# One transformer block with 32 experts on one core: a ring of eleven places in two rows, programs written out, the first norm done together, last transfers in halves

## What is computed

```python
h = h + token_mixer(rmsnorm(h, norm_mix_w[l]), w_in[l], ...)
h = h + moe_ffn(rmsnorm(h, norm_ffn_w[l]), w_router[l], b_router[l], w_mlp1[l], b_mlp1[l], w_mlp2[l], b_mlp2[l])
return rmsnorm(h, norm_final_w)
...
top_val, top_idx = lax.top_k(logits, TOP_K)          # 4 of 32 experts for each token
def expert_block(args):
    xb, e = args
    hdn = xb @ w_mlp1[e] + b_mlp1[e]                 # 1024 -> 2 x 1024
    glu = jnp.minimum(hdn[:, :D_FF], SWIGLU_LIMIT)
    lin = jnp.clip(hdn[:, D_FF:], -SWIGLU_LIMIT, SWIGLU_LIMIT)
    act = glu * jax.nn.sigmoid(SWIGLU_ALPHA * glu) * (lin + 1.0)
    return act @ w_mlp2[e] + b_mlp2[e]               # 1024 -> 1024
```

## Time and profile before

| | before |
|---|---|
| median of 3 runs | 1125.63 us (1125.26 to 1127.12) |
| the profiled execution | 1125.41 us, of it a span of 1123.6 us |
| TensorE (PE) busy | 1085.1 us, 97% |
| VectorE, ScalarE busy | 33%, 22% |
| bytes read | 437.67 MB |
| granted TensorE clock | 0.998 |

### The profile page before, as it was taken

How to read it: one execution, slowest core, us unless ns; L and a number is a source line. 1 busy time by engine, 2 the same in 40 slices (tenths; PEclk the granted TensorE clock), 3 DMA queues, 4 the chain that set the end, 5 groups by cost and what they waited for, 6 DMA issues and landing times.

```text
span 1123.6 us, 14458 instructions
## 1 busy us (share of the span) xinstructions
PE 1085.1 (97%) x5409; PEld 487.5 (43%) x5410; DVE 367.8 (33%) x813; ACT 245.6 (22%) x345; POOL 3.6 (0%) x12
## 2 busy tenths in 40 slices
PE   9999999999999999999999999999999999999996
PEld 8888888533333333333333333333333333333332
DVE  5977787422222222222222222222222222212223
ACT  4845674311111111111111111111111111111112
POOL 0000000000000000000000000000000000000000
PEclk9999999999999999999999999999999999999999
DMA  9655469999999999999999999999999999999996
GB/s 336 223 157 165 155 204 417 428 420 416 428 427 436 430 430 429 432 428 433 435 432 395 429 433 435 433 432 432 430 429 430 433 435 432 432 432 430 426 423 253
DMA packets 37877, 439.15 MB, mean 391 GB/s; under 512 B 5244, under 2 KB 5432, under 8 KB 21880
## 3 DMA queue, kind: packets, MB, share of 16 engines
q1 hardware_dynamic: 37488, 437.78, 93.3%
q10 hardware_dynamic: 360, 0.95, 0.3%
HBM read 437.67 MB, written 1.05 MB: 390 GB/s over the span
## 4 chain that ended last, share of the span: by engine, by line
PE 79%; DMA 14%; DVE 6%; issue 0%; ACT 0%; SPq 0%; DVEq 0%; PEldq 0%; ACTq 0%
PE bank L1154 33%; PE bank L1181 18%; DMA ring<-in_w_mlp_dram 11%; PE bank L798 9%; DMA late_slots<-in_w_mlp_dram 4%; PE bank L1083 3%; PE bank L1165 2%; PE bank L792 2%; PE bank L963 2%; PE bank L1011 2%; DVE xn L1670 2%; DVE xn L1667 2%; DVE xn L1674 2%; PE bank L1059 1%; PE bank L1067 1%; PE bank L1133 1%
## 5 line engine op out<-in xcount | busy, mean ns | idle before, releaser
L1154 PE MATMUL bank<-ring,xn 128*64 128x512 f32 x1232 | 276.3, 595 | 6.3 <-DMA ring<-in_w_mlp_dram 6.3
L1154 PE MATMUL bank<-late_slots,xn 128*64 128x512 f32 x880 | 197.5, 596 | 4.9 <-DMA late_slots<-in_w_mlp_dram 4.9
L1154 PEld LDWEIGHTS bank<-ring,xn 128*64 128x64 f32 x1232 | 84.4, 136 | 163.8 <-issue 150.3
L1181 PE MATMUL bank<-ring,smo 128*64 128x512 f32 x624 | 138.3, 595 | 0.0
L705 ACT ACTIVATE xn<-bank 128x512 f32<-128x512 f32 x33 | 19.7, 598 | 481.5 <-PE bank L1154 481.5
L1154 PEld LDWEIGHTS bank<-late_slots,xn 128*64 128x64 f32 x880 | 60.2, 136 | 117.9 <-issue 106.3
L1683 DVE SCALAR_TENSOR_TENSOR moe_y_lo<-bank,st,moe_y_hi 128x512 fp32r<-128x512 f32 x33 | 24.8, 750 | 235.5 <-ACT moe_y_hi L712 235.5
L1667 DVE TENSOR_SCALAR xn<-bank 128x512 f32<-128x512 f32 x33 | 22.8, 691 | 220.9 <-PE bank L1154 220.9
L1181 PE MATMUL bank<-late_slots,smo 128*64 128x512 f32 x416 | 92.1, 595 | 0.0
L1181 PEld LDWEIGHTS bank<-ring,smo 128*64 128x64 f32 x624 | 42.9, 137 | 81.1 <-issue 81.1
L712 ACT ACTIVATE moe_y_hi<-bank,st 128x512 fp32r<-128x512 f32 x33 | 22.7, 687 | 233.7 <-PE bank L1181 233.7
(11 more groups left out here) (270 smaller groups left out, 890.9 us busy)
## 6 DMA issues: line engine op xcount, KB each, us to landing
ring<-in_w_mlp_dram SPq DMA_DIRECT2D x43, 4096.0 KB, 30.4
late_slots<-in_w_mlp_dram SPq DMA_DIRECT2D x29, 4096.0 KB, 28.0
ring<-in_w_mlp_dram SPq DMA_DIRECT2D x28, 2048.0 KB, 13.4
late_slots<-in_w_mlp_dram SPq DMA_DIRECT2D x15, 2048.0 KB, 15.6
ring<-in_w_in_dram SPq DMA_DIRECT2D x22, 1024.0 KB, 5.4
late_slots<-in_w_mlp_dram SPq DMA_DIRECT2D x8, 1024.0 KB, 38.5
ring<-in_w_branch_dram SPq DMA_DIRECT2D x4, 1024.0 KB, 5.0
ring<-in_w_out_dram SPq DMA_DIRECT2D x4, 1024.0 KB, 7.1
```

The costliest lines, as they stand in the source:

```text
L1154: last = mm(B[4 + u][g * C:(g + 1) * C, :], xgT[:, k % 4, k // 4, :], by_group(held[k // 2][0][:, k % 2, u * FF:(u + 1) * FF], g), start=F ...
L1181: last = mm(B[7][g * C:(g + 1) * C, :], actT[:, j, h * C:(h + 1) * C], held[4 + h][0][:, j // 2, (j % 2) * D + g * N:(j % 2) * D + (g + 1) ...
```

## The change

1. **Eleven places.** `late_slots` grows by two slots (its end lies over the tile `sga`, whose content is dead by then), `PLACES` becomes 11, `place_used_once` goes, and chunk `m` lies in place `m % 11`. A load waits for the chunk 11 before it, not 10.
2. **Which chunks go in one transfer.** The places lie in two rows, places 10, 0, 1, 2, 3 in `late_slots` and 4 to 9 in `ring`. A transfer of 4 MB needs its two places side by side in one row, so chunk `m` and its follower go singly where `m % 11` is 3 or 9. Of the 72 transfers of 4 MB 58 are left, and 14 become two of 2 MB.
3. **First loads.** Still eleven before the first item, behind the same waits, in another order.
4. **Programs written out.** No rounds: TensorE and SP have each expert's code once, one after the other. Counts are constants. `scatter_b2` moves to before expert 16.
5. **First norm together.** Mean, root and reciprocal of both halves of the tokens in one instruction each; the second scaled copy goes to ScalarE. 12 fillers in place of 14.
6. **Last pieces in halves.** The second pieces of chunks 3 and 5 of expert 31 are loaded as two transfers of 0.5 MB, and TensorE waits for each.
7. **Fillers.** Experts 28 and 29 run 4 filler matmuls ahead of their third chunk.
8. **Last norm.** The mean of the second half is worked out between the two output pieces of the first.

```diff
-PLACES = 10
-ROUND = PLACES // 2
-QUADS = range(ROUND + 1, E - 2)
+FIRST_QUADS = 6
+PLACES = 11
+QUADS = [m for m in range(CHUNKS * FIRST_QUADS, CHUNKS * (E - 2), 2) if m % PLACES not in (3, PLACES - 2)]
...
-        places = [late_pair[1], pair[0], pair[1], pair[4], pair[5], pair[2], pair[3], late_pair[2], late_pair[3], late_pair[0]]
-        quads = {1: ring[:, 0:4, :], 3: ring[:, 8:12, :], 5: ring[:, 4:8, :], 7: late[:, 4:8, :], 9: late[:, 0:4, :]}
+        places = late_pair[1:5] + pair + late_pair[0:1]
+        quads = {n: late[:, at:at + 4, :] for n, at in ((PLACES - 1, 0), (0, 2), (1, 4), (2, 6))}
+        quads.update({4 + n: ring[:, 2 * n:2 * n + 4, :] for n in range(5)})
...
-                    for half, done in enumerate((place_landed[place], piece_landed[i])):
-                        sp.dma_start(places[place][:, half, :], src[:, half * SLOT:(half + 1) * SLOT]).then_inc(done, 16)
+                    at = [0, SLOT, 2 * SLOT] if i % 2 == 0 else [0, SLOT, SLOT + FF, 2 * SLOT]
+                    for a, b, done in zip(at, at[1:], (place_landed[place], piece_landed[i], half_landed.get(i))):
+                        sp.dma_start(places[place].rearrange("p a n -> p (a n)")[:, a:b], src[:, a:b]).then_inc(done, 16)
...
+            for e in range(E - 1):
+                after = sp.value_load(first_item[0:1, e + 1:e + 2], min_val=1, max_val=ITEMS - 1)
+                for i in range(CHUNKS):
+                    m = CHUNKS * e + i + PLACES
+                    if m >= CHUNKS * E:
+                        continue
+                    if m not in QUADS and m - 1 not in QUADS:
                         wait_freed(after, i)
+                        load(m // CHUNKS, m % CHUNKS, m % PLACES, 2 if m >= CHUNKS * (E - 1) + 2 else 1)
+                    elif m - 1 in QUADS:
                         wait_freed(after, i)
+                        load_quad(m // CHUNKS, m % CHUNKS // 2, (m - 1) % PLACES)
...
-                for t in range(TT):
-                    act.wait_ge(meansq, t + 1)
-                    nc.scalar.activation(st[:, 4 + t:5 + t], st[:, 2 + t:3 + t], ACT.Sqrt).then_inc(root, 1)
+                act.wait_ge(meansq, TT)
+                nc.scalar.activation(st[:, 4:4 + TT], st[:, 2:2 + TT], ACT.Sqrt).then_inc(root, TT)
...
+            act.wait_ge(rstd, TT)
+            nc.scalar.activation(xn[:, 1, :], xs[:, 1, :], ACT.Copy, scale=st[:, 7:8]).then_inc(xn_ready, 1)
...
-            keep_warm(14, hm[:, :, :, :].rearrange("p t h d -> p (t h d)"))
+            keep_warm(12, hm[:, :, :, :].rearrange("p t h d -> p (t h d)"))
...
                     if k == 4:
+                        keep_warm(fill, tables)
                         turn_gates(3 * i + 5)
...
                     for u in range(2):
+                        if u and k == KB - 1 and 3 in in_halves:
+                            pe.wait_ge(*in_halves[3])
...
+            for e in range(1, E - 1):
+                if e == E // 2:
+                    pe.wait_ge(opened, 2 * TT)
+                    scatter_b2()
+                first = after
+                after = pe.value_load(first_item[0:1, e + 1:e + 2], min_val=1, max_val=ITEMS - 1)
+                with pe.Fori(first, after) as i:
+                    item(i, chunks(e), fill=4 if E - 6 < e and CHUNKS * e not in QUADS and CHUNKS * e + 2 in QUADS else 0)
...
-            final_scale(0)
+            final_rstd(0)
+            final_half(0, 0)
             final_mean(1)
-            final_scale(1)
+            final_half(0, 1)
+            final_rstd(1)
+            final_half(1, 0)
+            final_half(1, 1)
```

More of the change, by code:

```diff
@@ L115, in landings @@
     for m in range(CHUNKS * E):
[L116 to L121, removed]
+        place = m % PLACES
+        if m - 1 in QUADS:
             table.append(table[-1])
@@ L418, in _ @@
             sp.wait_ge(slots_used, Q_OUT + 2)
[L419 to L420 removed]
+            first_load(1)
+            first_load(6)
             sp.wait_ge(slots_used, Q_MOE)
[L422 to L424 removed]
+            first_load(2)
+            first_load(7)
+            first_load(10)
             sp.wait_ge(firsts, 1)
[L427 to L431 removed]
@@ L433, in pieces @@
-            def pieces(m):
-                return 2 if m >= CHUNKS * (E - 1) + 2 else 1
-            def refill(e, c, chunks, whole, whole_second):
-                after = sp.value_load(first_item[0:1, bass.ds(e + 1, 1)], min_val=1, max_val=ITEMS - 1)
-                for i in range(chunks):
-                    m = CHUNKS * c + i
-                    if not (whole_second if i < 2 else whole):
+            for e in range(E - 1):
[5 more added lines that the diff above has]
+                    if m not in QUADS and m - 1 not in QUADS:
@@ L1101, in chunks, with item @@
             def chunks(e):
[L1103 to L1122 removed]
+                at = [(m, *landing[m]) for m in range(CHUNKS * e, CHUNKS * (e + 1))]
+                return [(places[m % PLACES], place_landed[place], 16 * count) for m, place, count in at]
             def by_group(columns, g):
                 return columns.rearrange("p (q g s) -> p g q s", g=2, s=ROWS)[:, g]
[L1128 removed]
+            def item(i, held, in_pieces={}, in_halves={}, fill=0):
                 pe.wait_ge(row_ready, i + 1)
@@ L1234, in _ @@
             dve.wait_ge(sumsq, TT)
-            for t in range(TT):
-                norm(t)
-                v.tensor_scalar(xn[:, t, :], xs[:, t, :], st[:, 6 + t:7 + t], None, ALU.mult).then_inc(xn_ready, 1)
+            v.tensor_scalar(st[:, 2:2 + TT], st[:, 0:TT], 1.0 / D, EPS, ALU.mult, ALU.add).then_inc(meansq, TT)
+            dve.wait_ge(root, TT)
+            v.reciprocal(st[:, 6:6 + TT], st[:, 4:4 + TT]).then_inc(rstd, TT)
+            dve.wait_ge(rstd, TT)
+            v.tensor_scalar(xn[:, 0, :], xs[:, 0, :], st[:, 6:7], None, ALU.mult).then_inc(xn_ready, 1)
             dve.wait_ge(rows_turned, 1)
```

125 lines of the change are left out of this document (37 added, 88 removed).

## The result

The changed kernel takes 1128.15 us (median of 21 runs, 1126.17 to 1130.22), the kernel before 1125.70 (median of 21 runs beside them). The ratio is 1.0017, with a 95% interval of 1.0011 to 1.0023: about 1.9 us slower. That is just inside the 0.2% that was called no change, though the plain difference of the medians is 2.45 us and 1128.15 lies just over the 1127.9 from which the prediction said slower. The profiled execution took 1126.42 us, of it a span of 1124.6, so it stands 1.0 over the profiled one of before and 1.7 under its own kernel's median.

A forecast was written before the change was run, and what follows sets the result against it. The stream of weight transfers was taken as the longer chain, bounding the kernel. Terms -1.0 + 1.0 + 0 + 3.4 - 1.2 - 0.3 = +1.9 on the profile's 1125.41 gave 1127.3 us, range 1122.9 to 1130.2.

The forecast's parts named there:

- First norm and fillers: At the head, transposes start at 8.9 in place of 9.91, so the weight stream starts 1.0 us earlier: -1.0.
- Fourteen splits: In the weight stream, 14 transfers of 4 MB become two of 2 MB each, 0.07 us apiece: +1.0.
- The eleventh place: Near 600 the DMA stall of 1.76 us on the engines' average goes, but no landing moves: 0.
- Programs written out: Experts 11 to 30: about 20 more code fetches disturb the weight stream, 0.17 us each: +3.4, between 0.8 and 12.
- The late fetch: At expert 31's last piece, the landing made 1.2 us late by one code fetch is no longer hit: -1.2.
- Halves: At expert 31's last pieces, halves save up to 0.9 us only if the piece is late, which it isn't: 0.
- Fillers: At experts 28 and 29, four fillers of 1.95 us hide in the wait for the third chunk: 0.
- Last norm: At the end, VectorE's 0.42 us wait for the second root now lies behind an output piece: -0.3.
- the engines even out: Rival, chance 0.27: in the weight stream fetches cost their bytes, 0.8 us in all, the stall's 1.8 count as gain; 1122.9.
- 0.39 for a fetch: Rival, chance 0.15: each code fetch costs the weight stream the average of both early stretches, +7.7 for 3.4; 1131.6.
- a gap for each split: Rival, chance 0.02: each of 14 splits in the weight stream costs 1.2 us, 17 in place of 1.0; 1143.
- The head's gain is lost on the way: Rival, chance 0.06: the 1.0 us gained at the head does not reach the time; +2.9, 1128.3.

The follow-up runs named there:

- e12: The kernel before with only the gates' small matmuls broken in two groups; 1125.70 us, ratio 0.9998.
- e5: The kernel before with the first norm of both halves together, 12 fillers for 14, and the gates' small matmuls in two groups; 1124.54 us, ratio 0.9988.
- e4: The changed kernel with every chunk loaded by a transfer of its own, 58 more splits; 1131.66 us, ratio 1.0048 to the kernel before.
- e6: The changed kernel with each load waiting for the chunk ten before it, from the first refill on; 1130.62 us, ratio 1.0045 to the kernel before.
- e9: The changed kernel with loads from chunk 16 on waiting for the chunk ten before, not eleven; 1128.60 us, ratio 1.0023 to the kernel before.
- e7: The kernel before with the first norm together, last pieces in halves and the last norm reordered; 1125.33 us, ratio 0.9991.
- e11: The kernel before with TensorE's program written out for experts 6 to 15, the loop kept for 16 to 30; 1127.43 us, ratio 1.0015.
- e2: The kernel before with TensorE's program of experts 6 to 30 written out in place of the loop; 1129.04 us, ratio 1.0029.
- e1: The changed kernel without the four fillers at experts 28 and 29; 1128.48 us, ratio 1.0018 to the kernel before.
- e8: The changed kernel with the gates' small matmuls broken in two groups; 1127.17 us, ratio 1.0012 to the kernel before.
- e3: The kernel before with the first norm of both halves together and 12 fillers in place of 14; 1125.61 us, ratio 0.9992.

## Why the prediction held, and where it did not

The forecast was 1127.3, the likeliest class no change that can be told, at 0.45; it came out at 1128.15. The main step, that new code costs the stream some 0.17 us a fetch, was right. That the number came so close is in part luck: the two profiles are 1.0 apart and not 1.9 (the last wait for a third chunk came 2.97 later and not 3.4, the way behind it got 1.41 shorter and not 1.2, the end 0.56 and not 0.3), and the medians are 2.45 apart, while no step had runs at a lower mean clock than the profiled one's. By its steps:

1. **First norm and fillers, -1.0.** Right in size: 1.09 in the chain from x to the transposes, 1.2 between the medians of e12 and e5. (Over all profiles that chain is 4.06 to 4.87 in four without the change and 3.32 to 3.87 in ten with it.) Not whole in the time: in the profile x landed 0.59 later, and in many executions the clock falls behind the gates' matmuls. The step "PE has no wait from there to the first load, so the stream starts 1.0 us earlier" passed over that: no wait, but another clock.
2. **Fourteen splits, +1.0.** Right: 0.076 each in e4.
3. **The eleventh place, 0.** Right for the stall near 600 as the kernel before, e6 and e9 show it; e5 and e7 lost 2.5 us there, so in some executions the eleventh place gives that too. Wrong as a whole. The step that failed is also the one ahead of it: the 4.2 us too much from 174.2 to 349.6 were all put down to fetches and the mixer, because I cut no window there. 1.2 of them are a second stall at 250 that the eleventh place takes away, 1.1 to 2.0 at the waits of e9.
4. **Programs written out, +3.4.** Right: 22 fetches, 0.17 to 0.19 each in e11 and e2, so 3.7 to 4.2. The changed kernel's third chunk is waited for 2.97 us later than before; the terms as measured are -0.5 + 1.0 - (1.1 to 2.0) + (3.7 to 4.2), 2.2 to 3.6.
5. **The late fetch, -1.2.** Right: no wait at the last piece in the changed kernel or in e2. What hits a landing late is a matter of where the fetches fall: e12, with the loop, has it again (1.05 at 1101.92), e5 has not, and e4 and e6 have a fetch in 1097 to 1100 but no wait at the last piece.
6. **Halves, 0.** Not tried apart from the last norm. The profile says about 0.4: a whole piece would have landed with its second half, at 1103.0, and PE was ready for it at 1102.62. That is an estimate from these two times; step 5's "ready at the same moment" was not quite so.
7. **Fillers, 0.** Right in time (e1).
8. **Last norm, -0.3.** A bit more: from the start of L1044's group at 1102.78 to the span's end are 20.8 us before, and from 1104.34 (now L1034) 20.3 after.

In the profiles this closes: the last third-chunk wait 2.97 later, less 1.41 on the way to that group (1.20 of it the late piece), less 0.56 at the end, is 1.0, and the spans differ by 1.0. The other 1.4 us of the medians' difference are not in this profile: 18 of the changed kernel's 21 runs had a mean clock of 0.996 or less, its profiled one 0.997. e8 gives back 1.0 of it, as far as its interval tells; for the rest the falls behind the long waits (916.14 above, 5.29 in place of 3.65) are the likely place, but no profile shows one that cost time in the changed kernel itself.

Of the rivals, "the engines even out" is excluded: the cost of 22 fetches is 4 and not 0.8 us. It had one thing right, that the eleventh place is worth something, mostly at another place than it said. 0.39 for a fetch is excluded by e2 and e11 (0.19 and 0.17), a gap for each split by e4. "The head's gain is lost on the way" came true by half in the profile, 0.5 of 1.0.

## What to carry to other kernels

Where one stream of transfers is the longer chain, a landing is as late as its latest engine: what costs the average little (an instruction fetch, 1.4 / 22 = 0.06 us on the mean of sixteen) can cost it three times that, and what costs the average much (a stall of engines that are ahead) can cost it nothing, or, as e5 and e7 show, 2.5 us. Keep the code of the long-running engine in a loop that it has already fetched, and when a stretch is slower than its rate, cut windows in it before giving it one cause. A median above its own profile is worth a look at the mean clocks of the runs: a profile that happened on full clock says nothing of the ones that did not.

## What the runs showed of the hardware that was not expected

- **Fetches spread the engines.** At the third chunk of expert 29 the sixteen engines finish their parts within 0.86 us in the kernel before and 8.0 us apart in the changed one: eight parts lie within 2.4 us of the first and eight 6.4 to 8.0 behind it, as if half of the engines took all fetches and the others ran ahead. Before, a stall had made them level again near 600 (4.2 us apart ahead of it, 0.8 behind), at no cost to the landings.
- **One engine can be late behind a stall.** In two of ten profiles with the stall near 600 one of the sixteen parts came 2.1 to 2.5 us behind the other fifteen, and the whole stream behind it was 2.5 us later; why is open.
- **The clock falls while TensorE is busy.** 2.1 us of matmuls and transposes with 4 rows, between full ones and with no idle time, were followed by a granted clock of 0.50 to 0.61 in 40:42 in three profiles (e3, e7, e9) and of 1.00 in seven (before, changed, e1, e2, e4, e6, e11); in e3 the fall cost 1.54 us. In two groups with 2.1 us of full matmuls between, it was seen in none of 33 runs' mean clocks.
- **Waits of the same length end either way.** Behind 2.17 us (e1 at 916.64) the next 16 matmuls took 3.65, behind 2.18 (945.85) 5.35; in e8 waits of 2.25 and 2.29 were followed by full clock.
